# Half-frequency filter spectra and forward transforms, with a re-ordered branch, in a two-block float32 kernel

## The reference

```python
u_h = short_conv3(u_h, conv_w[l], conv_b[l])
hv, hx1, hx2 = jnp.split(u_h, 3, axis=-1)
filt = hyena_filters(S, flt_w1[l], ..., flt_deltas[l])
z = fft_long_conv(hv, filt[:, 0], flt_bias[l, 0]) * hx1
z = fft_long_conv(z, filt[:, 1], flt_bias[l, 1]) * hx2
y_h = z * jax.nn.silu(z_h)
...
def fft_long_conv(u, h_f, bias):
    y = jnp.fft.irfft(jnp.fft.rfft(u32, n=2 * L, axis=1) * h_f[None], n=2 * L, axis=1)[:, :L]
    return (y + u32 * bias.astype(jnp.float32)).astype(u.dtype)
```

## Time and profile before

| | |
|---|---|
| median of three runs | 2069.11 us |
| profiled execution, its own time | 2067.41 us |
| its span, first to last instruction | 2065.6 us |
| TensorE busy (matmul) | 1998.3 us |
| VectorE, ScalarE, GpSimd busy | 659.8, 379.0, 111.1 us |
| mean granted TensorE clock | 0.985 |

### The profile page before, as it was taken

How to read it: one execution, slowest core, us unless ns; L and a number is a source line. 1 busy time by engine, 2 the same in 40 slices (tenths; PEclk the granted TensorE clock), 3 DMA queues, 4 the chain that set the end, 5 groups by cost and what they waited for, 6 DMA issues and landing times.

```text
span 2065.6 us, 28841 instructions
## 1 busy us (share of the span) xinstructions
PE 1998.3 (97%) x12128; PEld 1104.6 (53%) x12128; DVE 659.8 (32%) x1436; ACT 379.0 (18%) x784; POOL 111.1 (5%) x94
## 2 busy tenths in 40 slices
PE   6999999999998999999989988999999999999998
PEld 5577775667774865777756544232323333333332
DVE  3265113345212474344449934010101010111112
ACT  3212103212102232243320012010101010111101
POOL 0000000000000000000016610000000000000000
PEclk9999999999999999999999998999999999999999
DMA  8245575344665223243323125989898979797973
GB/s 316 82 163 204 217 282 202 116 156 171 234 265 228 82 82 150 115 175 131 123 102 123 41 102 217 376 329 374 324 384 330 381 309 403 311 402 298 406 299 148
DMA packets 41645, 472.71 MB, mean 229 GB/s; under 512 B 4676, under 2 KB 6340, under 8 KB 8040
## 3 DMA queue, kind: packets, MB, share of 16 engines
q1 hardware_dynamic: 39008, 465.44, 56.6%
q10 hardware_dynamic: 2568, 6.31, 0.9%
HBM read 470.68 MB, written 1.06 MB: 228 GB/s over the span
## 4 chain that ended last, share of the span: by engine, by line
PE 88%; DVE 7%; DMA 3%; issue 1%; ACT 0%; ACTq 0%; SPq 0%; POOLq 0%; POOL 0%; DVEq 0%
PE bank L898 21%; PE bank L551 14%; PE bank L928 11%; PE bank L850 7%; PE bank L862 3%; PE bank L714 3%; PE bank L543 3%; PE bank L536 3%; PE bank L720 3%; PE bank L564 2%; PE bank L978 2%; PE bank L970 2%; DMA arena<-in_wgu 1%; PE bank L617 1%; PE bank L649 1%; PE bank L1074 1%
## 5 line engine op out<-in xcount | busy, mean ns | idle before, releaser
L898 PE MATMUL bank<-arena 128*32 128x512 f32 x4096 | 453.1, 594 | 1.7 <-DMA arena<-in_wgu 1.7
L551 PE MATMUL bank<-arena 128*128 128x256 f32 x1408 | 312.6, 381 | 0.0
L898 PEld LDWEIGHTS bank<-arena 128*32 128x32 f32 x4096 | 130.3, 110 | 311.1 <-issue 296.3
L551 PEld LDWEIGHTS bank<-arena 128*128 128x128 f32 x1408 | 264.9, 190 | 53.7 <-issue 19.4
L928 PE MATMUL bank<-arena 128*32 128x512 f32 x2112 | 238.2, 595 | 0.0
L1993 DVE TENSOR_TENSOR arena<-arena,bank 128x256 f32<-128x256 f32 x64 | 27.0, 421 | 595.3 <-ACT arena L1406 540.4
L850 PE MATMUL bank<-arena 128*128 128x256 f32 x704 | 153.7, 379 | 0.1
L850 PEld LDWEIGHTS bank<-arena 128*128 128x128 f32 x704 | 133.6, 190 | 21.7 <-issue 4.1
L928 PEld LDWEIGHTS bank<-arena 128*32 128x32 f32 x2112 | 63.0, 110 | 133.2 <-issue 132.5
L1406 ACT ACTIVATE arena<-bank 128x256 f32<-128x256 f32 x64 | 24.5, 383 | 587.9 <-PE bank L898 587.9
L2207 POOL TENSOR_TENSOR arena<-arena 128x512 f32<-128x512 f32 x64 | 81.2, 1268 | 293.0 <-DVE arena L2040 290.5
(11 more groups left out here) (416 smaller groups left out, 1952.6 us busy)
## 6 DMA issues: line engine op xcount, KB each, us to landing
arena<-in_wgu SPq DMA_DIRECT2D x88, 2048.0 KB, 9.4
arena<-in_w SPq DMA_DIRECT2D x46, 2048.0 KB, 8.1
arena<-in_wdn SPq DMA_DIRECT2D x88, 1024.0 KB, 7.9
arena<-in_modw SPq DMA_DIRECT2D x24, 2048.0 KB, 10.2
arena<-in_wf SPq DMA_DIRECT2D x11, 3072.0 KB, 10.3
arena<-in_flt_deltas ACTq DMA_DIRECT2D x2, 1024.0 KB, 15.6
cst<-in_consts SPq DMA_DIRECT2D x1, 1162.0 KB, 17.3
arena<-in_x SPq DMA_DIRECT2D x1, 1024.0 KB, 5.3
```

Source lines behind the costliest of these rows:

```text
L551: ins = mm(bank[b][:, j * S:(j + 1) * S], w[:, col:col + P], hT[:, k, :], start=(k == 0), stop=(k == KT - 1))
L898: ins = mm(bank[w % 2][32 * j:32 * j + 32, :], hTe[:, k, TOK * b:TOK * b + TOK], wslot[c % RING][:, k, :], start=(k == 0), stop=(k == KT - ...
```

## The change

A filter spectrum or a signal spectrum is now summed over even tokens (tile 0) and odd tokens (tile 1) apart, and only at 128 of the 256 frequencies. Their sum is the spectrum of one half, their difference, read in mirrored order of frequencies, that of the other. For this:

- The filter network's output and the signal's transposes read every second column (`c::2`, `t::2`), so that a tile holds the tokens of one parity; the tables are laid out by parity, the inverse tables mirrored in their second half.
- `f_spec` has 4 matmuls a filter in place of 8. ScalarE copies the two even banks, VectorE forms sum and difference with the odd banks (four instructions of 512 columns).
- `dft` has 2 matmuls a step in place of 4. Step h=0 writes the even sums, which ScalarE copies to `even`; step h=1 waits for that copy and adds the odd sums in the same banks. VectorE does nothing at h=0. At h=1 it does the product of half 0, two SCALAR_TENSOR_TENSOR that form 2*even minus the whole, and the product of half 1.
- In `after`, `mix` comes ahead of the `dft` of h=1 behind HX1's first half; `idft` of order 1 and the second `turn` come later by a projection or more, so do the second `dft` pair and the `idft` of order 2.
- Some semaphores are merged: the transfers of decay rates and filter weights share one, those of the masks and `ffw` another, and two waits of ScalarE on itself use its chain.

```diff
-        8: [("dft", 0, 1), ("mix", 0, 0)],
-        9: [("weigh", 0, 0), ("idft", 0, 0), ("scores", 1, 0)],
-        10: [("turn", 1, 0), ("mix", 1, 0), ("values", 0, 0)],
-        11: [("weigh", 1, 0), ("dft", 1, 0), ("scores", 2, 0)],
-        12: [("dft", 1, 1), ("mix", 2, 0), ("values", 1, 0)],
-        13: [("weigh", 2, 0), ("scores", 3, 0)],
+        8: [("mix", 0, 0), ("dft", 0, 1)],
+        9: [("weigh", 0, 0), ("scores", 1, 0)],
+        10: [("mix", 1, 0), ("idft", 0, 0), ("values", 0, 0)],
+        11: [("weigh", 1, 0), ("turn", 1, 0), ("scores", 2, 0)],
+        12: [("mix", 2, 0), ("dft", 1, 0), ("values", 1, 0)],
+        13: [("weigh", 2, 0), ("dft", 1, 1), ("scores", 3, 0)],
         14: [("mix", 3, 0), ("values", 2, 0)],
-        15: [("weigh", 3, 0), ("idft", 1, 0)],
-        16: [("values", 3, 0)],
+        15: [("weigh", 3, 0)],
+        16: [("values", 3, 0), ("idft", 1, 0)],
...
+        even = view(big1 + 2048, 2, 512)
...
-                            mm(bank[4 + q][:, :], fa[0:64, 2, c * P:(c + 1) * P],
+                            mm(bank[4 + q][:, :], fa[0:64, 2, c::2],
...
                     elif name == "f_spec":
 
                         pe.wait_ge(sm["fold_ready"], l + 1)
-                        for kt in range(2):
+                        if c == 1:
+                            pe.wait_ge(sm["fp_done"], l * 4 + 2)
+                        for t in range(TT):
                             for ri in range(2):
-                                q = 2 * kt + ri
-                                if c == 1:
-                                    pe.wait_ge(sm["fp_done"], l * 8 + q + 1)
-                                for t in range(TT):
-                                    lhs = (FCt, FSt)[ri][:, t, kt * P:(kt + 1) * P]
-                                    rhs = hf[:, t, c, :] if ri == 0 else hn[:, t, c, :]
-                                    ins = mm(bank[4 + q][:, :], lhs, rhs, start=(t == 0), stop=(t == TT - 1))
-                                ins.then_inc(sm["fp_ps"], 1)
+                                src = (hf, hn)[ri][:, t, c, :]
+                                mm(bank[4 + 2 * t + ri][:, :], (FCt, FSt)[ri][:, t, 0:P], src,
+                                   start=True, stop=True).then_inc(sm["fp_ps"], 1)
...
-                                                          src[:, j, t * P:(t + 1) * P], ident)
+                                                          src[:, j, t::2], ident)
...
                     elif name == "dft":
 
                         if h == 0:
                             pe.wait_ge(sm["utok_ready"], l * 4 + 2 * c + 2)
                         else:
-                            pe.wait_ge(sm["spec_ready"], l * 4 + 2 * c + 1)
+                            pe.wait_ge(sm["du_ready"], l * 4 + 2 * c + 2)
                         for ri in range(2):
-                            for t in range(TT):
-                                ins = mm(bank[2 + ri][:, :], (FCt, FSt)[ri][:, t, h * P:(h + 1) * P], utok[:, t, :],
-                                         start=(t == 0), stop=(t == TT - 1))
+                            ins = mm(bank[2 + ri][:, :], (FCt, FSt)[ri][:, h, 0:P], utok[:, h, :],
+                                     start=(h == 0), stop=True, skip_group_check=True)
...
-                            pe.wait_ge(sm["fp_done"], l * 8 + 8)
+                            pe.wait_ge(sm["fp_done"], l * 4 + 4)
...
-                        for q in range(4):
-                            act.wait_ge(sm["fp_ps"], l * 8 + 4 * c + q + 1)
-                            F(H[:, c, q // 2, q % 2, :], bank[4 + q][:, :], ACT.Copy).then_inc(sm["fp_done"], 1)
+                        for ri in range(2):
+                            act.wait_ge(sm["fp_ps"], l * 8 + 4 * c + ri + 1)
+                            F(H[:, c, 1, ri, :], bank[4 + ri][:, :], ACT.Copy).then_inc(sm["fh_ready"], 1)
+                    elif name == "dft" and h == 0:
+                        act.wait_ge(sm["dft_ps"], l * 4 + 2 * c + 1)
+                        for ri in range(2):
+                            F(even[:, ri, :], bank[2 + ri][:, :], ACT.Copy).then_inc(sm["du_ready"], 1)
...
                     elif name == "dft":
-                        if c == 0 and h == 0:
-                            dve.wait_ge(sm["fp_done"], l * 8 + 8)
-                        dve.wait_ge(sm["dft_ps"], l * 4 + 2 * c + h + 1)
-                        C, Sn = bank[2][:, :], bank[3][:, :]
-                        re, im = H[:, c, h, 0, :], H[:, c, h, 1, :]
-                        link(v.tensor_tensor(tmp[:, 0, :], C, re, ALU.mult))
-                        link(v.tensor_tensor(tmp[:, 1, :], Sn, im, ALU.mult))
-                        link(v.tensor_tensor(Y[:, h, 0, :], tmp[:, 0, :], tmp[:, 1, :], ALU.add))
-                        link(v.tensor_tensor(tmp[:, 0, :], Sn, re, ALU.mult))
-                        link(v.tensor_tensor(tmp[:, 1, :], C, im, ALU.mult))
-                        v.tensor_tensor(Y[:, h, 1, :], tmp[:, 0, :], tmp[:, 1, :], ALU.subtract).then_inc(sm["spec_ready"], 1)
-                        dve.wait_ge(sm["spec_ready"], l * 4 + 2 * c + h + 1)
+                        if h == 0:
+                            continue
+                        dve.wait_ge(sm["du_ready"], l * 4 + 2 * c + 2)
+                        dve.wait_ge(sm["dft_ps"], l * 4 + 2 * c + 2)
+                        for half in range(2):
+                            re, im = H[:, c, half, 0, :], H[:, c, half, 1, :]
+                            if half == 0:
+                                C, Sn = bank[2][:, :], bank[3][:, :]
+                            else:
+
+                                C, Sn = even[:, 0, :], even[:, 1, :]
+                                link(v.scalar_tensor_tensor(C, C, 2.0, bank[2][:, :], ALU.mult, ALU.subtract))
+                                link(v.scalar_tensor_tensor(Sn, Sn, -2.0, bank[3][:, :], ALU.mult, ALU.add))
+                            link(v.tensor_tensor(tmp[:, 0, :], C, re, ALU.mult))
+                            link(v.tensor_tensor(tmp[:, 1, :], Sn, im, ALU.mult))
+                            link(v.tensor_tensor(Y[:, half, 0, :], tmp[:, 0, :], tmp[:, 1, :], ALU.add))
+                            link(v.tensor_tensor(tmp[:, 0, :], Sn, re, ALU.mult))
+                            link(v.tensor_tensor(tmp[:, 1, :], C, im, ALU.mult))
+                            v.tensor_tensor(Y[:, half, 1, :], tmp[:, 0, :], tmp[:, 1, :], ALU.subtract).then_inc(sm["spec_ready"], 1)
+                            dve.wait_ge(sm["spec_ready"], l * 4 + 2 * c + half + 1)
+                    elif name == "f_spec":
+                        for ri in range(2):
+                            dve.wait_ge(sm["fh_ready"], l * 4 + 2 * c + ri + 1)
+                            dve.wait_ge(sm["fp_ps"], l * 8 + 4 * c + 2 + ri + 1)
+                            whole, alias, odd = H[:, c, 0, ri, :], H[:, c, 1, ri, :], bank[6 + ri][:, :]
+                            link(v.tensor_tensor(whole, alias, odd, ALU.add))
+                            ab = (alias, odd) if ri == 0 else (odd, alias)
+                            v.tensor_tensor(alias, ab[0], ab[1], ALU.subtract).then_inc(sm["fp_done"], 1)
+                            dve.wait_ge(sm["fp_done"], l * 4 + 2 * c + ri + 1)
...
-    tneg = _np.stack([-lin[:P], -lin[P:]], 1)
-    parts = [_np.eye(P), _np.eye(P)[::-1], _np.ones((P, P)), tiles(fc), tiles(fs), tiles(fc.T / S), tiles(fs.T / S),
+    tneg = _np.stack([-lin[0::2], -lin[1::2]], 1)
+    by_parity = lambda m: _np.concatenate([m[0::2], m[1::2]])
+    mirrored = lambda m: _np.concatenate([m[:P], m[P:][::-1]])
+    parts = [_np.eye(P), _np.eye(P)[::-1], _np.ones((P, P)), tiles(by_parity(fc)), tiles(by_parity(fs)),
+             tiles(mirrored(fc.T / S)), tiles(mirrored(fs.T / S)),
```

More of the change, by code:

```diff
@@ L334, in model @@
         wmix = [ring[0], ring[1], ring[0], ring[1], view(LOW + 4096, CH), view(W + 5376, CH)]
-        names = """x_landed cst_landed rest_landed ev_landed row_landed row_ps row_ready row_stored biasr_landed
-                bias_ps bias_ready vec_landed delta_landed fwo_landed post_landed
+        names = """x_landed cst_landed rest_landed ev_landed row_landed row_ps row_stored biasr_landed
+                bias_ps bias_ready vec_landed filter_landed post_landed
                 act_chain dve_chain pool_chain ms_ready std_ready xn_ready xt_ps ht_ready x_ready
                 lam_in lam_ps lam_exp f_ps f_arg f_sine fo_ps fo_decay fo_used fold_ready
-                fp_ps fp_done grp_ps even_free odd_free turn_ps utok_ready dft_ps spec_ready
-                idft_ps z_ready sc_ps sc_ready pr_ready wg_ready wt_ps wt_ready va_ps va_used
+                fp_ps fh_ready fp_done grp_ps even_free odd_free turn_ps utok_ready dft_ps spec_ready
+                du_ready idft_ps z_ready sc_ps sc_ready pr_ready wg_ready wt_ps wt_ready va_ps va_used
                 on_ready yt_ps ya_ready
```

(21 more changed lines are left out.)

3 lines of the change are left out of this document (1 added, 2 removed).

## The result

The change made the kernel slower by 0.28%. Nineteen runs of each gave a median of 2077.6 us after and 2072.25 us before; the ratio is 1.0028 with a 95% interval of 1.0018 to 1.0038. The forecast was 2073.9 us against a median of 2069.11, which is +4.8 us; the ratio makes it +5.8 us (+3.7 to +7.9), and the profiled executions (2067.41 and 2073.88 us) stand 6.47 us apart. The median of 2077.6 us is 3.7 us above the forecast, but 3.1 us of that stand in the kernel before as well, whose nineteen runs have a higher median than the three that the forecast started from.

What follows compares the result with a forecast made beforehand. TensorE was taken to bound the kernel (busy 97% of the span, 88% of the chain). Terms: -27.5 - 0.4 + 14.4 + 11.1 + 7.2 = +4.8 us, forecast 2073.9 us, range 2066 to 2079 us.

Steps and rivals of the forecast that it cites:

- matmuls halved: TensorE's filter spectrum steps and forward transforms take half as long, all of it on the chain: -27.5 us.
- weighing of head 0: Its transposes no longer wait for `mix`, which now comes before the transform on VectorE: 0.2 us a layer, -0.4 us.
- first hold: TensorE waits 7.2 us before HX2's first half until VectorE's convolution frees bank 0: 14.4 us per kernel.
- second hold: TensorE waits 5.54 us before ZH's second half until ScalarE's modulation copy frees bank 1: 11.1 us per kernel.
- clock: TensorE works at half speed after each of four waits, 1.8 us lost each: +7.2 us (6.0 to 8.4).
- strided weights: Loading every second column as weights in turns and filter outputs costs 0, bounds 0 and +4.5 us.
- VectorE in the filter steps, the copies, the merged semaphores: Sums and differences, ScalarE's copies and merged load waits lie under other work or come early: counted as 0.
- The piece: VectorE's unbroken spectrum block, both halves' products and two SCALAR_TENSOR_TENSOR of 512 columns: 4.35 + 4.35 + 1.57 = 10.27 us.
- (a): Rival: TensorE's clock stays at its upper level in the waits; 2066.7 us, no measurable change; chance 0.20.
- (b): Rival: larger waits, from slow strided loads (+4.5 us) or longer half speed (+1.1); 2078 to 2079.5 us; chance 0.14.
- (c): Rival: the order hides VectorE's spectrum block at HX2 and ZH, only -27.9 us remain; 2041.2 us; chance 0.08.

Runs made afterwards that it cites:

- e4: The changed kernel with dft h=1 of both orders moved later and values 0 ahead of the inverse transform; 2041.35 us, ratio 0.9861 against the kernel before.
- e1: The changed kernel with 8 and 6 constant matmuls put into each layer's two idle places of TensorE; 2069.33 us, ratio 0.9997 against the kernel before.
- e8: e4 with the turns' transposes and the filter outputs reading dense columns again, so the branch's values are not the reference's; 2041.46 us, one run.
- e7: e1 with 5 and 3 constant matmuls in place of 8 and 6, so part of the idle time stays; profiled execution 2072.06 us, one run.

## Why the prediction was right, point by point

The sign, the places and the forecast's size were right; the terms, against what they measured in the profiled executions:

| term | predicted us | measured us | from |
|---|---|---|---|
| matmuls halved | -27.5 | -27.5 | steps of 3.43 and 1.72 us |
| weighing of head 0 | -0.4 | -0.4 | its wait is not among TensorE's |
| first hold, twice | +14.4 | +14.2 | 7.12 each |
| second hold, twice | +11.1 | +10.7 | 5.32 and 5.33 |
| clock | +7.2 | +8.5 | 17.1 us at 0.50 |
| strided weights | 0 | +0.4 | a turn of 0.96 us for 0.87, four turns |
| sum | +4.8 | +5.9 | |
| profiled executions apart | | +6.5 | |

- **Matmuls.** Right to 0.01 us a step, and e4 shows that the gain is real when nothing waits: -28.8 us by the ratio, -25.5 us by the profiles.
- **VectorE in the filter steps, the copies, the merged semaphores.** Counted as nothing; e4 has all of them and no wait of TensorE in the branch but 0.9 us.
- **The piece.** Predicted 10.27 us, measured 10.15. The step that was off is the choice of rows for the SCALAR_TENSOR_TENSOR of 512 columns: the line through them gave 0.785 us with its gap, and the timeline has 0.69, with its gap 0.725, as every TENSOR_TENSOR beside it. Two of them make 0.12 us, which is the piece's whole difference. The line itself was right for its kind: both of its rows multiply by a column of a tile, and such an instruction of 512 columns took 751 ns in the kernel before (L2090). The two new ones multiply by a constant. Of that kind the kernel before had 418 ns at 256 columns (L1577, on 64 partitions) and 958 ns at 768 (L1763), and a line through these gives 688 ns at 512; L1608 took 686.
- **The holds.** The two sums (19.2 - 11.98 and 16.44 - 10.90) were right in their releasers and to 0.1 and 0.2 us in size. At the second, 0.12 us is the piece, and 0.25 us for the hand-over from ScalarE, taken from another place, was too much: the chain has 0.04 there. Against both, VectorE started 0.12 us behind the transform (176.37 to 176.49) and not 0.04.
- **The clock.** The step was right in kind and small in size: 1.8 us a hold from two rows with 2.99 and 4.17 us at half speed; the four measured 3.61, 5.49, 5.14 and 2.84, on average 4.3 us, so 2.1 us a hold. The sum of 8.5 lies just above my upper end of 8.4. The Trainium skill, "TensorE: Matmul & The Clock Gate", section "Part 1: The HAM clock gate", calls the slow clock the default from which activity releases the engine; the trace agrees, as the clock was 0.50 behind all four holds and 1.00 in e1, where TensorE had work in them.
- **Strided weights.** I took 0 of bounds 0 to 4.5. The loads are longer by half (209 ns for 141), but most of it lies under the passes beside them: a turn of eight transposes lasts 0.96 us for 0.87. The Trainium skill, "SBUF — State Buffer", section "Door 1: The DMA port swizzle", made it exactly 0, as two hits in a 16-byte line keep full bandwidth. For TensorE's weight loads e8 shows otherwise, and the measurement decides. Of its 4.5 us upper bound a tenth came true.
- **Rivals.** (a), a clock that stays up, is refuted by the four windows at 0.50. (b), larger holds or loads, is true in its part on the clock, 1.3 us, and in a tenth of its part on the loads. (c), that the holds are hidden, was wrong for this kernel, but its 2041.2 us is what e4 ran in (2041.35): the condition was not the length of the piece but its place.

One term is missing from the sum: a hold also undoes the overlap of neighbouring matmuls. The chain counts 1.85 us for the modulation product and 0.89 for the values, where the timeline has 1.92 and 1.05; each projection behind a hold thus starts 0.07 or 0.16 us later than the sum has it, 0.5 us in the four. That is nearly the 0.6 us between the sum and the profiled executions, though outside the branch smaller differences of both signs stand against each other. What is open is why the clock held in one of e7's four places.

## What to carry to other kernels

When work is moved from the bounding engine to one with slack, ask for its room ahead of each result that is due, not for its busy share: VectorE was idle for two thirds of the span and had 7.2 us of room ahead of the convolution, and it came 7.1 us late. Count both sides, as the shorter work of the bounding engine brings the due time nearer; here that took more of the room than VectorE's longer block. Then look what stands behind the block in its queue and which buffer that frees; here three steps, moved by one place each, were worth 1.7% with not one instruction changed. Price an idle time of TensorE at its length and half of the slow work behind it, here 2 us more each.

## What the runs showed of the hardware

- Idle time of 2.63 to 2.75 us on TensorE was enough, in three of four cases, for the clock to fall from 1.00 to 0.50; in the kernel after, 2.84 to 5.49 us of dense projections behind the four holds ran at the lower clock. In e7's first place it fell only some 1 us after TensorE had resumed at 130.47: 1.00 until 131.4, then 0.50.
- In the turns, a 128x128 float32 weight load with every second column took 209 ns instead of 140; with 64 rows (the filter outputs) it took 193 instead of 187 ns.
- A float32 SCALAR_TENSOR_TENSOR with a constant factor took 418, 686 and 958 ns at 256, 512 and 768 columns; with a column of a tile as its factor it took 484, 751 and 1286 ns at 256, 512 and 1024. At 512 columns the former (one operand in PSUM) took as long as a TENSOR_TENSOR.
